# Norms on whole tiles: sums of squares by a matrix of ones in place of single columns that are spread again

## The reference, cut to what matters

```
def _layer_norm(x, g, b):                       # after every mixer and every MLP, 9 in all
    mu = jnp.mean(xf, axis=-1, keepdims=True)
    var = jnp.mean(jnp.square(xf - mu), axis=-1, keepdims=True)
    y = (xf - mu) * lax.rsqrt(var + LN_EPS)
    return (y * g + b)
def _rms_norm(x):                               # even mixer (4 heads), retention (4), HGRN2 (4)
    return xf * lax.rsqrt(jnp.mean(jnp.square(xf), axis=-1, keepdims=True) + RMS_EPS)
```

## Time and profile before

| | |
|---|---|
| median of 3 runs | 2759.46 us |
| the profiled execution, its own time | 2754.0 us |
| span of its trace (first to last instruction) | 2752.2 us |
| mean granted TensorE clock | 0.992 |
| products on PE, records | 16362 |
| reciprocals of `recip` / roots of `root` | 29 / 29 |

### The profile page before, as it was taken

One profiled execution on the slowest core, in us unless ns is written; L12 is line 12 of the kernel. 1 busy time (PEld: TensorE's weight loads), 2 busy tenths in 40 slices (PEclk: granted clock), 3 DMA queues, 4 the chain that ended last, 5 costly groups with the idle time before them and its releaser, 6 DMA issues.

```text
span 2752.2 us, 39526 instructions
## 1 busy us (share of the span) xinstructions
PE 2692.2 (98%) x16362; PEld 2349.6 (85%) x16362; DVE 1267.9 (46%) x2178; ACT 1016.7 (37%) x1621; POOL 275.5 (10%) x350
## 2 busy tenths in 40 slices
PE   8999999999999999999999999999999999999997
PEld 7888999999987879788888988888888887888887
DVE  5544654333432323573334533435666654633333
ACT  4545443222332223352223432323566543522222
POOL 0000300001200000220000310012211130300002
PEclk9999999999999999999999999999999999999998
DMA  3111243222111212332222132222322222332220
GB/s 141 54 47 47 78 138 104 91 92 78 47 62 62 92 62 77 100 106 94 92 100 92 65 131 94 85 94 75 108 85 69 77 68 79 94 112 92 100 69 31
DMA packets 67683, 232.94 MB, mean 85 GB/s; under 512 B 9008, under 2 KB 11440, under 8 KB 67120
## 3 DMA queue, kind: packets, MB, share of 16 engines
q1 hardware_dynamic: 67504, 230.41, 25.2%
HBM read 228.25 MB, written 2.10 MB: 84 GB/s over the span
## 4 chain that ended last, share of the span: by engine, by line
PE 88%; DVE 4%; ACT 3%; POOL 2%; issue 2%; DMA 1%; DVEq 0%; SPq 0%; POOLq 0%; ACTq 0%
PE ps L590 77%; PE ps L904 2%; PE ps L1030 1%; PE ps L600 1%; POOL R L2685 1%; PE ps L783 1%; POOL S L2670 1%; PE ps L743 1%; PE ps L891 1%; ACT HT L1265 1%; DVE HT L1927 1%; DVE R L1934 1%; PE ps L610 1%; PE ps L1127 1%; PE ps L623 0%
## 5 line engine op out<-in xcount | busy, mean ns | idle before, releaser
L590 PE MATMUL ps<-XH,WH 128*128 128x264 f32 (+2 forms) x1856 | 537.1, 331 | 12.9 <-DVE XL L2644 7.9
L590 PE MATMUL ps<-XH,LENT 128*128 128x512 f32 (+2 forms) x2096 | 526.5, 341 | 3.3 <-DVE XL L1951 3.2
L590 PE MATMUL ps<-XL,WH 128*128 128x264 f32 (+2 forms) x1856 | 523.2, 324 | 0.0
L590 PE MATMUL ps<-XH,WL 128*128 128x264 f32 (+2 forms) x1856 | 522.5, 324 | 0.0
L590 PE MATMUL ps<-HH,LENT 128*128 128x264 f32 (+2 forms) x2220 | 490.5, 318 | 1.9 <-DVE LENT L1905 1.9
L1905 DVE TENSOR_TENSOR WL<-RAW,WH 128x1024 fp32r<-128x1024 f32 (+1 forms) x232 | 286.3, 1234 | 264.0 <-ACT WH L1234 263.4
L590 PEld LDWEIGHTS ps<-XH,LENT 128*128 128x128 f32 x2096 | 355.7, 189 | 53.4 <-DVE XL L1951 4.5
L590 PEld LDWEIGHTS ps<-HH,LENT 128*128 128x128 f32 x2220 | 361.1, 190 | 32.1 <-DVE LENT L1905 2.3
L590 PEld LDWEIGHTS ps<-XH,WH 128*128 128x128 f32 x1856 | 318.8, 189 | 54.0 <-issue 12.7
L590 PEld LDWEIGHTS ps<-XH,WL 128*128 128x128 f32 x1856 | 318.5, 189 | 28.1
L590 PEld LDWEIGHTS ps<-XL,WH 128*128 128x128 f32 x1856 | 318.8, 189 | 26.7
(11 more groups left out here) (216 smaller groups left out, 2661.3 us busy)
## 6 DMA issues: line engine op xcount, KB each, us to landing
RAW<-in_wf SPq DMA_DIRECT2D x128, 512.0 KB, 3.3
RAW<-in_wr SPq DMA_DIRECT2D x48, 512.0 KB, 3.2
RAW<-in_wg SPq DMA_DIRECT2D x44, 512.0 KB, 3.2
RAW<-in_wu SPq DMA_DIRECT2D x44, 512.0 KB, 3.3
RAW<-in_wd SPq DMA_DIRECT2D x32, 512.0 KB, 3.2
RAW<-in_we SPq DMA_DIRECT2D x24, 512.0 KB, 3.3
RAW<-in_wm SPq DMA_DIRECT2D x24, 512.0 KB, 3.2
RAW<-in_wro SPq DMA_DIRECT2D x16, 512.0 KB, 3.2
```

The costliest lines, as they stand in the source:

```text
L590: mm = e.matmul(o[:, to:to + m], wt, xt[:, k, c0 + a * m:c0 + (a + 1) * m], start=(n == 0 and j == 0), stop=(n == nk - 1 and j == 2))
```

## The change

`stat` takes the matrix `ONE` of 128x128 ones as the stationary operand and the squares as the moving one: the sum stands in every row at once, over the token columns, in PSUM. `root` takes the root of the whole tile (128 rows and T columns) from PSUM to SBUF; `recip` makes the reciprocal of the whole tile in place. All `spread` products and their semaphore go. The multiplications read the tile `roots` in SBUF (`S1` for the layer norms, two slots of `HT` for the others) where they read PSUM before. In a layer norm the fill steps around `spread` are joined (4 + 9 become 13). In `hgrn` the copy to `y` goes. The new root waits until the last user of the tile before it is done.

```diff
-    def root_cols(key):
-        a = 64 + 12 * (ROOTS.setdefault(key, len(ROOTS)) % 2)
-        return SM[:, a:a + 12]
+    def roots(key, T):
+        ln, half = key
+        if ln in ("even", "ret", "hg"):
+            return HT[:, 0:2, :].rearrange("p a c -> p (a c)")[:, 0:T]
+        c = span(ln)[0] + half * T if ln != "mem" else 0
+        return S1[:, c:c + T]
...
-        def stat(key, srcs, T):
-            wd, n = chunks(T)
-            o = bank(("stat", key), 1, (S.root, *key))
+        def stat(key, srcs, T, at=range(8)):
+            pieces = [(0, HALF), (512, HALF)] if T == TW else [(0, T)]
+            o = bank(("stat", key), len(pieces), (S.root, *key), at=at)
             for i, (src, mark) in enumerate(srcs):
                 w.wait_ge(*mark)
-                for j in range(n):
-                    mm = e.matmul(o[0:wd, j:j + 1], src[:, wd * j:wd * j + wd], ONE[:, 0:1],
-                                  start=(i == 0 and j == 0), stop=(i == len(srcs) - 1 and j == n - 1),
-                                  skip_group_check=True)
+                for a, (to, m) in enumerate(pieces):
+                    mm = e.matmul(o[:, to:to + m], ONE[:, :], src[:, a * m:a * m + m],
+                                  start=(i == 0), stop=(i == len(srcs) - 1))
             mm.then_inc(*S.stat(*key))
-        def spread(key, T, freed, keep=True):
-            wd, n = chunks(T)
-            o = bank(("bcast", key), 2 if T == TW else 1, freed, keep=keep)
-            st = root_cols(key)
-            w.wait_ge(*S.recip[key])
-            for j in range(n):
-                at = wd * j if T != TW or j < 3 else 512 + wd * (j - 3)
-                mm = e.matmul(o[:, at:at + wd], st[0:wd, 6 + j:7 + j].broadcast_to([wd, 128]), ID[0:wd, 0:wd],
-                              start=True, stop=True)
-            mm.then_inc(*S.bcast(*key))
...
             pump(17 if beside_mem else 18)
-            rstd((ln, half), [(HT[:, 1, 0:T], S.add_pool[(ln, half, 4)]), (HT[:, 2, 0:T], S.add_dve[(ln, half, 7)])],
-                 T, (S.normed, ln, half, 7), pump, 3 if beside_mem else 4)
-            pump(9)
-            give(("bcast", (ln, half)))
+            stat((ln, half), [(HT[:, 1, 0:T], S.add_pool[(ln, half, 4)]), (HT[:, 2, 0:T], S.add_dve[(ln, half, 7)])], T)
+            pump(12 if beside_mem else 13)
...
-                    if i == 4 and 1 <= t <= 4:
-                        even_spread(t - 1)
                     even_back(5 * t + i, pump)
                     if i == 2 and 1 <= t <= 4:
-                        even_stat(t - 1)
+                        stat(("even", t - 1), [(TMP[:, 2, :], S.sq["even", t - 1])], TW, at=(0, 2))
...
-        def root(key, T, inv, ep):
-            wd, n = chunks(T)
-            st = root_cols(key)
+        def root(key, T, inv, ep, used):
             w.wait_ge(*S.stat[key])
             w.wait_ge(*S.const["eps"])
-            e.activation(st[0:wd, 0:n], acc(("stat", key), 1)[0:wd, 0:n], ACT.Sqrt, bias=eps[ep][0:wd, :],
+            if rooted[0]:
+                sig, *event = rooted[0]
+                w.wait_ge(*sig[tuple(event)])
+            rooted[0] = used
+            e.activation(two(roots(key, T), T), val(("stat", key), T), ACT.Sqrt, bias=eps[ep],
                          scale=inv).then_inc(*S.root(*key))
...
         def recip(key, T):
-            wd, n = chunks(T)
-            st = root_cols(key)
             w.wait_ge(*S.root[key])
-            e.reciprocal(st[0:wd, 6:6 + n], st[0:wd, 0:n]).then_inc(*S.recip(*key))
+            e.reciprocal(roots(key, T), roots(key, T)).then_inc(*S.recip(*key))
...
-                    w.wait_ge(*S.bcast[ln, half])
+                    w.wait_ge(*S.recip[ln, half])
...
-                    e.tensor_tensor(HT[:, T_SLOT[k], 0:T], res(k), spread, ALU.mult).then_inc(*S.normed(ln, half, k))
+                    e.tensor_tensor(HT[:, T_SLOT[k], 0:T], res(k), roots((ln, half), T), ALU.mult).then_inc(*S.normed(ln, half, k))
...
-            w.wait_ge(*S.bcast["hg", h])
-            e.tensor_copy(y, acc(("bcast", ("hg", h)), 1)).then_inc(*S.rms("hg", h))
-            w.wait_ge(*S.rms["hg", h])
+            w.wait_ge(*S.recip["hg", h])
+            w.wait_ge(*S.stat["hg", h])
             w.wait_ge(*S.par_in["par"])
-            e.scalar_tensor_tensor(y, acc(("hg_o", h), 1), pcol("hgn"), y, ALU.mult, ALU.mult).then_inc(*S.hg_dve("y", h))
+            e.scalar_tensor_tensor(y, acc(("hg_o", h), 1), pcol("hgn"), roots(("hg", h), 512), ALU.mult, ALU.mult).then_inc(*S.hg_dve("y", h))
```

More of the change, by code:

```diff
@@ L1267, in layer_norm @@
             pump(3)
-            root((ln, half), T, inv, LN_EPS)
+            root((ln, half), T, inv, LN_EPS, (S.normed, ln, half, 7))
             pump(5)
@@ L1486, in even @@
                     if i == 2 and 1 <= t <= 4:
-                        root(("even", t - 1), TW, 1.0 / 128, RMS_EPS)
+                        root(("even", t - 1), TW, 1.0 / 128, RMS_EPS, (S.scaled, "even", t - 1))
                 pump(100)
@@ L1944, in layer_norm @@
                 meanwhile()
-            spread = acc(("bcast", (ln, half)), 1)[:, 0:T]
             def lower(k):
```

48 lines of the change are left out of this document (11 added, 37 removed).

## The result

The changed kernel takes 2798.38 us, the median of 4 runs (2796.71 to 2799.44), where the kernel before took 2759.2 in the same session: a ratio of 1.0144, 95% interval 1.0132 to 1.0157. It is slower by 39 us. The forecast was 2769 with 2779 as its upper end. The direction was right, the size was off by 29 us, and the time lies outside the range.

What follows compares the result with a forecast made beforehand. PE, busy 98%, bounds the kernel, so the question is when a half's sixth `x_lo` comes. Terms from +12.6 (first halves) to -5.2 (hidden heads) sum to +9.9 us: 2763.9 profiled, 2769 on the median, range 2750 to 2779.

Steps and rivals of the forecast that it cites:

- The reciprocal's price: Wide reciprocal on DVE: 6 ns a column, so 1.6 us for 256 columns and 3.2 for 512 and 528.
- rival A: The wide reciprocal streams like a multiplication, 0.42 us for 256 columns: -11.3 us, 2748 us; chance 0.17.
- Rival C: Reciprocal at 8 ns a column and three or four more pieces at the lower clock: about 2780 us; chance 0.13.
- The products saved: PE products spared in all norms: 21.5 us if all counted, the most the change can bring through PE.
- Hgrn's last head: DVE works without a gap to the last low part, so the longer reciprocal and root cost +2.5 us.
- The last head of the retention: First scaled tile comes later behind the reciprocal and a panel's low part; PE waits all of it, +2.6 us.
- rival B: Reciprocal at 1.6 us but no loss beside POOL, step stays 0.80: -4.5 us, 2755 us; chance 0.2.
- with +0.25 each for DVE's 3.2 us ahead of the next scores: Even mixer, four heads: 1.5 us of products saved each, less 0.25 for the reciprocal's delay: -5.0 us.
- are hidden from DVE's delay by other panels: Three heads each of retention and hgrn save 0.87 us, with DVE's delay covered by other panels: -5.2 us.
- the second halves: Second halves of norms ln00 to ln3: small losses where PE waits, savings where fill is left: about -0.7 us.
- the operand in SBUF: Layer norm multiplications reading two SBUF inputs beside POOL: +0.27 us a tile, bounds 0 and +0.34.
- the clock: Idle time of PE brings at least one more piece at the lower clock: +1.7 us.

Runs made afterwards that it cites:

- r_all: Changed kernel with root and wide reciprocal replaced by one ScalarE activation giving the absolute reciprocal root: ratio 0.9926 to the kernel before, 20.4 us faster.
- n_even: Changed kernel with the reciprocal cut to 6 of 528 columns in the even mixer's four heads: ratio 1.0105 to the kernel before.
- n_hg: Changed kernel with the reciprocal cut to 6 of 512 columns in the four hgrn heads: ratio 1.0109 to the kernel before.
- m_both: Changed kernel with full-length reciprocals placed later in DVE's order, behind the key copy (even mixer) and first decay levels (hgrn): ratio 1.009 to the kernel before.
- n_ln0: Changed kernel, layer norms with root of a constant and a 6-column reciprocal in first halves only: ratio 1.0112 to the kernel before.
- n_ln: Changed kernel, layer norms with root of a constant and a 6-column reciprocal in both halves: ratio 1.0066 to the kernel before.

## Why the prediction was right and wrong

**Right.** The reciprocal's price (6.25 ns a column measured, 6 taken), and with it the fall of rival A (streaming) and of C's 8 ns. The 6 was picked from 3 to 11 by a single row, so some of it is luck. The products saved (21.5 at most; 21.1 by r_all). The hidden heads of the retention. Hgrn's last head (2.5 forecast, a wait of 2.87). The last head of the retention, up to the row: the reciprocal starts at 1138.03 in the changed kernel, the weight panel's part follows, and PE waits 2.45 us, though for that panel's part and not for the scaled tile:

```profile
1138.03 3.35 DVE L1876 RECIPROCAL HT<-HT 128x512 f32<-128x512 f32 x1 [2.00 <-ACT HT L1205]
...
1141.30 1.16 DVE L1864 TENSOR_TENSOR WL<-RAW,WH 128x1024 fp32r<-128x1024 f32 x1
1142.38 0.68 DVE L2257 TENSOR_TENSOR SCR<-SCR,HT 128x512 f32<-128x512 f32 x1
...
1142.52 0.50 PE L589 MATMUL ps<-HH,WH 128*128 128x512 f32 x1 [2.45 <-DVE WL L1864]
```

The stretch as a whole grew by 3.4 us and not by 5.0: PE's wait for POOL's sums ahead of ln10 fell from 3.25 to 0.95 us, which the sum had not taken back. And rival B (no loss beside POOL) is refuted by 9 to 13 us.

**Wrong, the step that failed: for the even mixer "with +0.25 each for DVE's 3.2 us ahead of the next scores", and for hgrn that the other heads "are hidden from DVE's delay by other panels".** These terms came to -5.0 and (with the last head) -0.1 and were +10.1 and +11.1, 26 of the 33 us that the sum missed. In place of 0.25 us PE waits 2.02 to 2.63 in each of the four heads, and in place of nothing 2.71 in each of hgrn's three; the rest of the two rows is the lower clock behind some of these waits. The earlier trace rows already showed the copy as the very next instruction, and who reads what it writes was not asked: the next scores. For the retention the same sentence on other panels held. The prediction even named this as what would make it wrong ("stops PE by several us a head") and gave it no price. n_even, n_hg and m_both show it.

**Wrong in size, the second halves (-0.7 together).** They were taken as covered by fill; n_ln0 against n_ln puts some 12 us on their reciprocals.

**Wrong in size, the operand in SBUF.** +0.27 us a tile in the first halves only; measured +0.13 to +0.15 a tile, but in all halves, and through POOL on the sums for the next half as well: 9 to 13 us. The 0.80 us that the forecast took as the step was one pair of tiles; from the second `x_lo` to the fifth the mean step was 1.07 before (1177.12 to 1180.32 us, three steps). That pair went to 0.88, the mean to 1.22 (1189.50 to 1193.15). The 1.8 us of a first half came near its measured 1.47 since the start was underrated (0.15 for 0.40, of which 0.1 is the root) and the step overrated.

**Wrong in size, the clock (+1.7).** 89 us at the lower level against 44, worth about 22 us of PE's busy time against r_all. It goes with the waits: r_all has the same products and 0.993. Some 22 us of it came on top of 36 us of waits. Rival C had three or four more pieces at the lower clock, and there are nine more ahead of the tail (15 for 6). So its 2780 us are nearest, but 7 of them are for a reciprocal of 8 ns a column that is not there, and it had nothing for the waits in the even mixer and in hgrn.
